# Two weight layouts per expert on TensorE, one expert after the other, and a ring of seven weight slots, in a decoder trunk with a mixture of experts

## The chip, the cores and the metric

The kernel runs on one core of one Trainium2 chip. The metric is the device time of one execution in microseconds; lower is better. Durations inside an execution come from one profiled execution, whose times are counted from its first instruction.

## The reference, cut to what matters

Two decoder layers work on 256 tokens of width 1024 in float32. Layer 0 has forgetting attention, layer 1 differential attention on shared keys and values; each ends in a mixture of 16 experts (grouped top 2) of hidden width 512.

```python
for l in range(2):
    ...                                     # ada parameters, attention, post-norm residual
    h = modulate(x, sh_f, sc_f)
    gates = ...                             # (256, 16), two non-zero entries in each row
    for e in range(16):
        a = silu(h @ w_gate[l, e]) * (h @ w_up[l, e])      # 1024 -> 512
        out = out + gates[:, e:e + 1] * (a @ w_down[l, e]) # 512 -> 1024
    x = post_norm_residual(x, out, g_f, ...)
```

Only the rows of h that were routed to an expert matter for it. The router's choices for the inputs of `setup_inputs()`, counted with the reference, are these numbers of tokens for experts 0 to 15:

| layer | tokens of experts 0 to 15 |
|---|---|
| 0 | 17 21, 18 24, 38 15, 38 21, 27 45, 84 40, 28 30, 37 29 |
| 1 | 43 18, 3 44, 16 9, 1 14, 44 38, 16 72, 25 33, 93 43 |

The commas part the pairs in which the kernel takes them. Ten experts of layer 0 and eight of layer 1 have at most 32 tokens; expert 10 of layer 0 and experts 11 and 14 of layer 1 have more than 64.

## The kernel before

**Weights.** All weights stream from HBM in pieces of 2 MB ([128, 4096] float32), issued by SP in one written order. A piece goes into one of `RING` = 6 slots of `ring`; in the expert stages two more slots, `spare` and `stream`, join. `SLOT` and `TURN` fix at build time which slot a piece takes: in the ring stages piece n takes the slot of piece n - 6, in the expert stages that of piece n - 8. SP issues piece n when the semaphore `used` of its slot says that the last piece there was read, and waits in order, so one full slot holds up all later pieces. An expert stage has 48 pieces, six for each pair of experts: gate and up of the first expert, gate and up of the second, then the two down matrices (numbers 6i to 6i + 5 for pair i). Pieces `RING` and `RING` + 1 of a stage also wait for `x_ready` and `res_mm`. In layer 0 the six slots before the expert stage hold the four pieces of `ada(3)`, read by `mod_product(3)` in the router's stage, and the two output projections.

**Routing and windows.** DVE's `route` makes one-hot selections, positions and tables; PE gathers the tokens, sorted by expert, into `xsT`. For each expert POOL's `window` copies 64 columns into `xw`. Tokens beyond 64 go through `overflow`, rounds of 32 in a loop whose count DVE, ACT, PE and POOL load from `tabn`. There POOL copies the window `oxw` and PE runs `gate_up_strips`: four strips of 32 output columns, two for gate and two for up, each with half of the contraction, folded together by a matmul with `fold_strips`.

**A pair on PE.** `gate_up` of the first expert (8 steps of two matmuls side by side on 64 columns each, two PE instructions for each float32 matmul), `gate_up` of the second; in its middle the four transposes of the first expert's result, so that ACT's sigmoid and DVE's `glu` of the first run beneath the second. Then four `add_back` matmuls of the pair before (L1737), the second's transposes, `down` of the first, the transposes of `put`, `down` of the second. DVE's `gated` multiplies the outputs by the adaLN gate into `y`, which the next pair adds back. After an expert stage PE needs `ada(4)`, the four pieces behind it in SP's order (`turn_stream(1)`, L1431), and after layer 1 the last norm and the store.

Lines: L498 expert loads, L618 and L613 POOL's overflow copies, L630 and L631 windows, L799 and L805 ACT's copies of gate and up, L802 and L808 sigmoids, L1225 `put_pair`, L1233 and L1235 `glu`, L1242 `gated`, L1247 to L1271 DVE's overflow, L1724 and L1725 `gate_up`, L1732 and L1733 `down`, L1746 and L1756 strips, L1773 fold, L1811, L1821 and L1828 transposes.

## Time and profile before

| | |
|---|---|
| median of 3 runs | 900.73 us (900.71 to 902.5) |
| span of the profiled execution | 899.3 us |
| PE busy | 834.7 us, 93% |
| DVE, ACT, POOL busy | 376.0, 127.1, 90.3 us |
| read from HBM | 302.49 MB |
| mean granted TensorE clock | 0.986 |

The profiled execution's own total is not listed; its span is 1.4 us below the median, and that is taken as what lies before the first and after the last instruction. A clock of 1.00 is 2.4 GHz and 0.50 is 1.2 GHz. The page cuts the span into 40 slices of 22.5 us; further views give the chain of work that ended last, the instructions in order of time, busy times by stretch, and groups by line.

### The profile page before, as it was taken

How to read it: one execution, taken by the hardware profiler on the slowest of the kernel's cores; microseconds unless marked ns; L12 is line 12 of the kernel's file. 1: busy time of each engine (PE TensorE's matmuls, PEld its weight loads, DVE VectorE, ACT ScalarE, POOL GpSimd, SP SyncE). 2: the span in 40 equal slices, each digit the busy share in tenths (PEclk: the TensorE clock that was granted, in tenths of full speed). 3: DMA queues.
4: the chain of work that ended last, by engine and by line, in shares of the span. 5: the costliest groups of instructions: out<-in, count | busy, mean ns of one | idle time of the engine just before them, and what ended most of it. 6: DMA issues, size and time to landing. Idle time of an engine off the chain costs nothing.

```text
span 899.3 us, 10792 instructions
## 1 busy us (share of the span) xinstructions
PE 834.7 (93%) x3730; PEld 393.0 (44%) x3730; DVE 376.0 (42%) x927; ACT 127.1 (14%) x341; POOL 90.3 (10%) x146
## 2 busy tenths in 40 slices
PE   6899999999998998899979999999999999889984
PEld 3584675435333333333328557654533333333331
DVE  2185867475211221222148688828521122212215
ACT  1001243011100000000010114611110000010010
POOL 1000000051110001011004000215111110000000
PEclk9999999999999999999999999999999999999998
DMA  8999982019999999999999799405499999999901
GB/s 352 431 421 426 399 329 95 1 59 431 426 428 426 425 427 426 427 426 426 425 384 419 299 426 425 175 0 213 163 406 424 428 424 427 426 427 426 392 12 47
DMA packets 23408, 304.59 MB, mean 339 GB/s; under 512 B 2720, under 2 KB 3232, under 8 KB 5280
## 3 DMA queue, kind: packets, MB, share of 16 engines
q1 hardware_dynamic: 22752, 303.14, 80.6%
q8 instruction: 47, 0.77, 0.3%
q10 hardware_dynamic: 576, 0.40, 0.1%
q14 instruction: 33, 0.27, 0.1%
HBM read 302.49 MB, written 1.05 MB: 338 GB/s over the span
## 4 chain that ended last, share of the span: by engine, by line
PE 68%; DMA 21%; DVE 8%; issue 2%; POOL 1%; ACT 1%; POOLq 0%; DVEq 0%; ACTq 0%
PE ps L1724 17%; DMA ring<-in_moe_w_up_dram 12%; PE ps L1732 7%; PE ps L1558 6%; PE ps L1529 6%; PE ps L1542 6%; PE ps L1642 5%; PE ps L1737 4%; DMA stream<-in_moe_w_up_dram 3%; DMA ring<-in_ada_w_dram 3%; DMA ring<-in_moe_w_down_dram 3%; PE ps L1453 1%; PE ps L1431 1%; PE ps L1705 1%; PE ps L1465 1%
## 5 line engine op out<-in xcount | busy, mean ns | idle before, releaser
L1724 PE MATMUL ps<-ring,hT 128*64 128x512 f32 x384 | 172.4, 599 | 11.8 <-DMA ring<-in_moe_w_up_dram 9.9
L1725 PE MATMUL ps<-ring,hT 128*64 128x512 f32 x384 | 172.7, 600 | 0.0
L1233 DVE TENSOR_TENSOR arena<-arena,ps 128x256 f32<-128x256 f32 x32 | 13.5, 421 | 233.8 <-ACT arena L802 126.8
L1724 PEld LDWEIGHTS ps<-ring,hT 128*64 128x64 f32 x384 | 51.1, 138 | 117.4 <-issue 117.4
L1732 PE MATMUL ps<-ring,arena 128*64 128x512 f32 x208 | 94.8, 599 | 0.0
L1733 PE MATMUL ps<-ring,arena 128*64 128x512 f32 x208 | 94.8, 598 | 0.0
L414 DVE SCALAR_TENSOR_TENSOR spare<-ring,csig,spare 128x512 f32<-128x512 f32 x112 | 86.1, 769 | 3.8
L1737 PE MATMUL ps<-arena 128*128 128x512 f32 x144 | 66.6, 605 | 3.2 <-DVE arena L1242 3.2
L1724 PE MATMUL ps<-spare,hT 128*64 128x512 f32 x128 | 58.9, 609 | 2.7 <-DMA stream<-in_moe_w_up_dram 2.5
L1725 PE MATMUL ps<-stream,hT 128*64 128x512 f32 x128 | 58.9, 610 | 0.0
L1529 PE MATMUL ps<-hT,ring 128*128 128x256 f32 x256 | 57.2, 386 | 1.5 <-ACT hT L680 1.5
L630 POOL COPY hT<-arena 128x512 f32 x32 | 19.7, 615 | 372.6 <-PE ps L1725 222.1
L1242 DVE TENSOR_TENSOR arena<-ps,gbc 64x512 f32<-64x512 f32 x64 | 43.9, 686 | 29.6 <-PE ps L1733 28.6
L1542 PE MATMUL ps<-ring,hT 128*128 128x512 f32 x128 | 55.9, 595 | 0.0
L1529 PEld LDWEIGHTS ps<-hT,ring 128*128 128x128 f32 x256 | 49.6, 194 | 8.5 <-ACT hT L680 1.6
L1725 PEld LDWEIGHTS ps<-ring,hT 128*64 128x64 f32 x384 | 51.2, 138 | 0.0
L1732 PEld LDWEIGHTS ps<-ring,arena 128*64 128x64 f32 x208 | 26.3, 136 | 48.9 <-issue 48.9
L1737 PEld LDWEIGHTS ps<-arena 128*128 128x128 f32 x144 | 25.9, 189 | 43.7 <-issue 43.7
L799 ACT ACTIVATE arena<-ps 128x512 f32<-128x512 f32 x16 | 9.6, 597 | 243.4 <-PE ps L1725 243.4
L1542 PEld LDWEIGHTS ps<-ring,hT 128*128 128x128 f32 x128 | 24.1, 190 | 30.8 <-issue 30.8
L1724 PEld LDWEIGHTS ps<-spare,hT 128*64 128x64 f32 x128 | 17.3, 140 | 38.7 <-issue 38.7
L587 POOL TENSOR_SCALAR st<-mv 128x1 f32<-128x1 f32 x8 | 1.8, 223 | 294.6 <-DVE mv L1064 294.6
(281 smaller groups left out, 1083.3 us busy)
## 6 DMA issues: line engine op xcount, KB each, us to landing
ring<-in_moe_w_down_dram SPq DMA_DIRECT2D x26, 2048.0 KB, 21.8
ring<-in_ada_w_dram SPq DMA_DIRECT2D x24, 2048.0 KB, 14.7
ring<-in_moe_w_gate_dram SPq DMA_DIRECT2D x24, 2048.0 KB, 18.4
ring<-in_moe_w_up_dram SPq DMA_DIRECT2D x24, 2048.0 KB, 21.3
spare<-in_moe_w_gate_dram SPq DMA_DIRECT2D x8, 2048.0 KB, 23.2
stream<-in_moe_w_up_dram SPq DMA_DIRECT2D x8, 2048.0 KB, 25.3
ring<-in_fox_w_in_dram SPq DMA_DIRECT2D x6, 2048.0 KB, 9.8
ring<-in_kv_ada_w_dram SPq DMA_DIRECT2D x4, 2048.0 KB, 13.8
```

The lines of the kernel that those rows point to most:

```text
L414: ins = alu.scalar_tensor_tensor(out=dst, in0=w[:, k, :], scalar=csig[:, k:k + 1], in1=dst, op0=ALU.mult, op1=ALU.add)
L630: link(g.tensor_copy(xw[:, j, :, 0:CAP], xsT[:, :, bass.ds(first, CAP)]))
L1242: d.tensor_tensor(out[lo:lo + CAP, half], ps[part_, bank, :], gbc[part_, 1, half], ALU.mult).then_inc(done, 1)
L1529: mm = t.matmul(ps[:, u % 4, 0:S], wcols(piece)[:, k, cc * P:(cc + 1) * P], src[:, k, :], start=(k == 0), stop=(k == KC - 1))
L1542: mm = t.matmul(ps[:, u % 4, :], hT[:, k, b * P:(b + 1) * P], wcols(piece)[:, k, :], start=(k == 0), stop=(k == KC - 1))
L1558: mm = t.matmul(ps[:, 7, 0:S], wcols(n)[:, k, (c % 4) * P:(c % 4 + 1) * P], src[:, k, :], start=(k == 0), stop=(k == KC - 1))
L1642: mm = t.matmul(ps[:, 2 * b + s_, :], oT[l][:, k, b * P:(b + 1) * P], wcols(n)[:, k, :], start=(k == 0), stop=(k == KC - 1))
L1724: t.matmul(ps[0:CAP, bank, :], lhs(k), wcols(ng)[:, k, :], start=(k == 0), stop=(k == KC - 1))
L1725: mm = t.matmul(ps[CAP:P, bank, :], lhs(k), wcols(nu)[:, k, :], start=(k == 0), stop=(k == KC - 1))
L1732: t.matmul(ps[0:CAP, bank, :], lhs(f), wdown(n)[:, f, 0:512], start=(f == 0), stop=(f == 3))
L1733: mm = t.matmul(ps[CAP:P, bank, :], lhs(f), wdown(n)[:, f, 512:D], start=(f == 0), stop=(f == 3))
L1737: return t.matmul(ps[:, 2 * b + q, :], lhs[:, b * P:(b + 1) * P], yy[:, q * 512:q * 512 + 512], start=False, stop=True, skip_group_check=True)
```

## The change

The ring gets a seventh slot, so a piece takes the slot of the piece seven before it, or nine before it in the expert stages. On PE each expert is now one chain: `gate_up`, add-backs or transposes of `put`, fold or transposes, add-backs, `down`; then the next expert. A table `tabl`, made in `route`, says which experts have more than 32 tokens. PE loads its entry and branches: these take the old instructions (64 columns), the others take strips of 32 columns in bank 4 or 5 and a fold by a 128-wide `folded`. Slots are released later in the chain: gate and up of the first expert by the first two add-backs, of the second by the `put` transposes and the fold. `put_pair` writes 8 half-wide pieces instead of 4. The copies into `oxw` move from POOL to DVE, and ACT and DVE do their parts in the new order. The routing tiles move into `arena`, and a scratch size is passed at the build.

```diff
--- before.py
+++ after.py
-RING = 6
+RING = 7
...
-        fold_strips = sb("fold_strips", [P, 2 * OCAP])
+        fold_strips = sb("fold_strips", [P, 2, CAP])
...
-        rt = sb("rt", [P, 11, NB * NE])
-        rg = sb("rg", [P, 6, 2 * 2 * 8])
-        rc = sb("rc", [P, 2, NB * NG * EG * EG])
+        rt = part(P, 11, NB * NE)
+        rg = part(P, 2, NB * NG)
+        rc = part(P, 2, NB * NG * EG * EG)
...
             def windows(l):
-                def overflow(i, j):
...
-                        with pool.Fori(b, b + n) as r:
-                            g.tensor_copy(oxw[:, :, 0:OCAP], xsT[:, :, bass.ds(lo, OCAP)]).then_inc(o_own, 1)
...
-                            pool.wait_ge(o_pe, r * 5 + 1)
...
                 def window(i, j, o):
-                    if i:
-                        spent(pool, N_MOE[l] + 6 * (i - 1) + 2 * j + 1)
+                    if i or l:
+                        pool.wait_ge(gu_mm[j], i + 8 * l)
...
@@ scalar, experts @@
+                    act.wait_ge(gu_mm[0], q + 1)
+                    a.activation(gu[:, 0, :], ps[:, 4, :], ACT.Copy).then_inc(gu_ev[0], 1)
                     overflow(i, 0)
-                    spent(act, n0 + 1)
-                    a.activation(gu[:, 0, :], ps[:, 4, :], ACT.Copy).then_inc(gu_ev[0], 1)
                     act.wait_ge(tg_mm[0], q + 1)
...
@@ vector, route @@
+                totals, past = rt[:, 7, 0:NE], rt[:, 7, NE:2 * NE]
+                link(d.tensor_tensor(totals, each[:, 0:NE], each[:, NE:2 * NE], ALU.add))
+                link(d.tensor_scalar(past, totals, float(OCAP), float(OCAP), ALU.is_gt, ALU.mult))
+                link(d.tensor_tensor(t3(2), pos[:, :, 0:NE], past.unsqueeze(1).broadcast_to([P, NB, NE]), ALU.subtract))
+                link(d.tensor_copy(tabl[:, :], past[0:1, :]))
...
-                link(d.tensor_tensor(tot, each[0:1, 0:NE], each[0:1, NE:2 * NE], ALU.add))
+                tot = totals[0:1, :]
...
@@ vector, experts: put_pair, overflow, pair loop @@
-                            d.tensor_scalar(put[:, b, j * CAP:(j + 1) * CAP], lane[:, :],
-                                            pos[:, b, bass.ds(i * 2 + j, 1)], gate[:, b, bass.ds(i * 2 + j, 1)],
+                            d.tensor_scalar(put[:, b, lo:lo + OCAP], lane[:, :], pos[:, b, e:e + 1], gate[:, b, e:e + 1],
                                             ALU.is_equal, ALU.mult).then_inc(putted, 1)
+                            d.tensor_scalar(put[:, b, lo + OCAP:lo + CAP], lane[:, :], second[:, b, e:e + 1],
+                                            gate[:, b, e:e + 1], ALU.is_equal, ALU.mult).then_inc(putted, 1)
...
+                            d.tensor_copy(oxw[:, :, 0:OCAP], xsT[:, :, bass.ds(lo, OCAP)]).then_inc(o_own, 1)
...
+                            d.tensor_copy(oxw[:, :, bass.ds(to, OCAP)], xsT[:, :, bass.ds(src_, OCAP)]).then_inc(o_win, 1)
...
                     overflow(i, 0)
                     put_pair(i)
                     glu(0, q)
+                    dve.wait_ge(sc_mm, i + (10 * l + 1))
+                    spent(dve, n0 + 4)
+                    gated(y, 0, 4, y_ev[0])
                     overflow(i, 1)
-                    glu(1, q)
-                    dve.wait_ge(sc_mm, i + (10 * l + 1))
                     dve.wait_ge(tp_mm, q + 1)
                     d.tensor_copy(putT[:, :], ps[:, 6, 0:S]).then_inc(tp_ev, 1)
-                    spent(dve, n0 + 4)
-                    gated(y, 0, 4, y_ev[0])
+                    glu(1, q)
...
@@ tensor, experts @@
+                def between(i, j, q, n0):
+                    if j == 0:
+                        pe.wait_ge(tp_ev, q + 1)
+                        pe.wait_ge(y_ev[1], (q + 1) * 2)
+                        add_back(0, 0, putT, y).then_inc(used[slot(n0)], 1)
+                        add_back(0, 1, putT, y).then_inc(used[slot(n0 + 1)], 1)
+                    else:
+                        pe.wait_ge(putted, (q + 1) * 8)
+                        for b in range(NB):
+                            mm = t.transpose(ps[:, 6, b * P:(b + 1) * P], put[:, b, :], ident[:, :])
+                            if b == 0:
+                                mm.then_inc(used[slot(n0 + 2)], 1)
+                        mm.then_inc(tp_mm, 1)
+                    pe.wait_ge(gu_ev[j], q + 1)
+                def ahead_of_down(i, j, q, n0):
+                    if j == 0:
+                        add_back(1, 0, putT, y)
+                        add_back(1, 1, putT, y).then_inc(sc_mm, 1)
+                    pe.wait_ge(at_r[j], q + 1)
+                    landed(pe, n0 + 4 + j)
...
+                    for j in range(2):
+                        pe.wait_ge(y_ev[j], (q + 1) * 2)
+                        landed(pe, n0 + 2 * j)
+                        landed(pe, n0 + 2 * j + 1)
+                        pe.wait_ge(xw_r[j], q + 1)
+                        large = pe.value_load(tabl[0:1, bass.ds(i * 2 + j, 1)], min_val=0, max_val=OCAP)
+                        with pe.If(large > 0):
+                            gate_up(i, j, lambda k: xw[:, j, k, 0:CAP], 4 + j, range(KC)).then_inc(gu_mm[j], 1)
+                            overflow(i, j)
+                            between(i, j, q, n0)
+                            for f in range(4):
+                                mm = t.transpose(ps[:, 4 + j, f * P:(f + 1) * P], gu[:, j, f * P:(f + 1) * P], ident[:, :])
+                                if j and not f:
+                                    mm.then_inc(used[slot(n0 + 3)], 1)
+                            mm.then_inc(tg_mm[j], 1)
+                            ahead_of_down(i, j, q, n0)
+                            down(i, j, lambda f: aT[:, j, f * CAP:(f + 1) * CAP], 4 + j).then_inc(used[slot(n0 + 4 + j)], 1)
+                        with pe.Else():
+                            gate_up_strips(i, j, xw[:, j, :, :], 4 + j).then_inc(gu_mm[j], 1)
+                            between(i, j, q, n0)
+                            for f in range(4):
+                                mm = t.matmul(ps[:, 4 + j, f * P:(f + 1) * P], gu[:, j, f * P:(f + 1) * P], folded,
+                                              start=True, stop=True)
+                                if j and not f:
+                                    mm.then_inc(used[slot(n0 + 3)], 1)
+                            mm.then_inc(tg_mm[j], 1)
+                            ahead_of_down(i, j, q, n0)
+                            down_strips(i, j, aT[:, j, :].rearrange("p (c s) -> p c s", c=4), 4 + j
+                                        ).then_inc(used[slot(n0 + 4 + j)], 1)
...
-    nc = _bacc.Bacc("TRN2", target_bir_lowering=False, num_devices=1)
+    nc = _bacc.Bacc("TRN2", target_bir_lowering=False, num_devices=1, dynamic_dma_scratch_size=1024)
```

## Rows read from the trace of the kernel before

**Rows 1.** The page: busy times, then GB/s in 40 slices of 22.5 us.
```profile
PE 834.7 (93%) x3730; PEld 393.0 (44%) x3730; DVE 376.0 (42%) x927; ACT 127.1 (14%) x341; POOL 90.3 (10%) x146
...
GB/s 352 431 421 426 399 329 95 1 59 431 426 428 426 425 427 426 427 426 426 425 384 419 299 426 425 175 0 213 163 406 424 428 424 427 426 427 426 392 12 47
```

**Rows 2.** The chain that ended last: start us, length us, what it waited on.
```profile
349.29 25.07 DMA ring<-in_moe_w_down_dram
...
433.99 26.35 DMA ring<-in_ada_w_dram
...
643.79 0.61 PE ps L1724
...
756.94 27.44 DMA ring<-in_moe_w_up_dram
...
885.58 1.97 PE ps L1737 x4
```

**Rows 3.** Busy time by stretch: PE, PEld, DVE, ACT, POOL, clock, DMA share, GB/s.
```profile
652.00:784.00 132.00, 129.48 (x566) 45.75 (x562) 30.00 (x75) 11.08 (x21) 13.11 (x22) 1.00 1.00 422
```

**Rows 4.** SP's queue in order of time: start us, length us, what was issued.
```profile
117.00 25.01 SPq L484 DMA_DIRECT2D ring<-in_fox_w_o_dram  x2
197.49 0.33 SPq L498 DMA_DIRECT2D ring<-in_moe_w_gate_dram  x1
...
642.91 0.33 SPq L498 DMA_DIRECT2D stream<-in_moe_w_up_dram  x1
651.76 0.33 SPq L498 DMA_DIRECT2D ring<-in_moe_w_gate_dram  x1
```

**Rows 5.** The chain again, transposes of the first expert in two pairs that follow.
```profile
680.38 0.59 PE ps L1811 x4
...
706.46 0.59 PE ps L1811 x4
```

**Rows 6.** One of these pairs in order of time, all engines, cut.
```profile
680.32 0.66 PE L1811 MATMUL ps<-ident,arena 128*128 128x128 f32 x4
...
681.88 0.42 DVE L1235 TENSOR_TENSOR arena<-arena,ps 128x256 f32<-128x256 f32 x1
...
692.14 0.44 PE L1828 MATMUL ps<-ident,arena 128*128 128x128 f32 x2
...
692.50 0.64 PE L1732 MATMUL ps<-ring,arena 128*64 128x512 f32 x1
...
695.99 0.59 PE L1724 MATMUL ps<-ring,hT 128*64 128x512 f32 x1
```

**Rows 7.** An overflow round of layer 1 in order of time, cut.
```profile
794.07 3.64 PE L1746 MATMUL ps<-ring,mrow 128*32 128x512 f32 x32
...
797.78 0.60 ACT L785 ACTIVATE mrow<-ps 128x512 f32<-128x512 f32 x1 [6.80 <-PE ps L1746]
...
798.51 1.10 PE L1773 MATMUL ps<-fold_strips,mrow 128*128 128x64 f32 x8 [0.80 <-ACT mrow L785]
...
806.24 3.70 PE L1737 MATMUL ps<-arena 128*128 128x512 f32 x8
```

**Rows 8.** Order of time: two waits for weights; then 1 us as in rows 3.
```profile
340.38 0.61 PE L1724 MATMUL ps<-ring,hT 128*64 128x512 f32 x1 [2.74 <-DMA ring<-in_moe_w_up_dram]
...
784.62 0.61 PE L1724 MATMUL ps<-ring,hT 128*64 128x512 f32 x1 [3.04 <-DMA ring<-in_moe_w_up_dram]
...
786.00:787.00 1.00, 1.00 (x5) 0.33 (x3) 0.00 (x0) 0.00 (x0) 0.00 (x0) 0.50 1.00 426
```

**Rows 9.** Order of time: two loaded branches, and the last overflow's down strips.
```profile
641.76 1.28 ACT L799 ACT_TABLE_LOAD   x1 [0.69 <-issue]
...
645.74 0.54 DVE L1225 TENSOR_SCALAR arena<-lane,pos,gate 128x64 f32<-128x64 f32 x2 [1.53 <-issue]
...
857.59 3.50 PE L1756 MATMUL ps<-ring,fold 128*32 128x512 f32 x16 [1.03 <-DVE fold L1267]
```

**Rows 10.** Order of time: DVE's third copy of gathered tokens in layer 1.
```profile
639.43 0.81 DVE L898 TENSOR_SCALAR arena<-ps,modc 128x512 f32<-128x512 f32 x1 [0.51 <-PE ps L1705]
```

114 lines of the change are left out of this document (38 added, 76 removed).

## The prediction

> **What bounds the kernel now.** I read the page first: PE is busy 93% of the span, and the transfers run at 424 to 428 GB/s through both expert stages [rows 1]. Both look full, so the chain of waits has to say which one ends last, and where. In layer 0 it is the transfers. The chain waits there on one piece of weights after another, on the first down matrix of pair 5 (lands at 374.36) and at the end on the last piece of `ada(4)` (433.99 + 26.35 = 460.34) [rows 2]. In layer 1 the wait that matters is at 756.94 + 27.44 = 784.38, when the up matrix of pair 5's second expert (piece 33 of 48) lands [rows 2]. Up to there the transfers run full [rows 3]; behind it PE is the bound until the last add-back at 885.58 [rows 2]. Between the layers (460 to 644) the chain is PE and DVE work and waits for no transfer.
>
> So two prices have to be kept apart: a piece of 2.097 MB at 426 GB/s takes 4.92 us, 29.5 us per pair [rows 1], and a pair on PE takes 706.46 - 680.38 = 26.1 us [rows 5]. PE is faster already. Work taken from PE is worth time only behind the last wait for weights, in pairs 5 to 7 of layer 1.
>
> **The seventh slot.** In layer 0 SP issues the second projection piece at about 142 (117.00 + 25.01), then waits to 197.49 for `mod_product(3)` to free a slot [rows 4]. The slices from 135 to 197 are nearly empty [rows 1]. With seven slots the first expert piece takes the slot of a query piece, the one that the projection got at 142, and lands in that gap. At 197.5 the queue is one piece ahead and stays so, because the stage is bound by transfers to its end: `ada(4)` lands at 455.4, 4.9 earlier, and layer 1 starts 4.9 earlier. The cover for this is that PE finishes the stage by 455. With the prices below: pair 5's first down matrix lands at 374.4 - 4.9 = 369.5, the rest of expert 10 and its round takes 13.4, expert 11 13.4, pairs 6 and 7 19 and 24, the last gating and add-backs 5.3, so 444.6 and eleven us of room. If PE came later than 455, the gain would shrink by the excess.
>
> **Start of layer 1.** PE starts at 643.79 [rows 2]; now 643.8 - 4.9 + 0.4 = 639.3. The 0.4 is for `route`: three more small DVE operations of 0.16 to 0.2 us with their links, 0.65 in all, ahead of the copies of gathered tokens; a later copy waits 0.51 for PE [rows 10], so part is hidden (bounds 0 and 0.65). Before, SP issued piece 8 at 651.76 [rows 4], 8.0 behind PE's start, when a slot came free. Now pieces 0 to 8 are in by then, and piece 9 waits for the first add-back: load and branch 0.5, `gate_up` 7.0, add-back 0.9, so 639.3 + 8.4 = 647.7. Before, it took 784.4 - 651.8 = 132.6 us from that issue to the landing 26 pieces later. The same count now runs from piece 9 to piece 34, pair 5's first down matrix: 780.3. One more stall: piece 11 waits for expert 1's `put` transposes at about 658.5, and the two pieces before it are read by 658.9, an issue taking some 1.4 us to move data; I add 1.1. Piece 34 lands at 781.5. Before, at 4.92 behind piece 33, it would have been 789.3.
>
> **Prices on PE.** `down` on 64 columns takes 695.99 - 692.50 = 3.5 us and `gate_up`, twice as many matmuls, 7.0; four transposes 0.7; eight add-back instructions 3.7, so half of them 1.8; from the transposes' end over sigmoid and `glu` to PE 1.4 (680.98 to 682.30, and a wake-up) [rows 6]. The strips were already measured in the overflow: 3.64 for gate and up, then 0.8 until ACT's copy frees PE, 1.1 for the fold; the whole round delays the add-backs by 12.2 (794.07 to 806.24) [rows 7]. Down strips I price at 1.9: the one row shown took 3.50 at half clock [rows 9], and half the columns' time of `down` is 1.75. The wider fold stays at 1.1 (8 instructions of 0.14; above, at most twice that). So a small expert saves 3.4 + 1.6 and pays 0.4 for the fold.
>
> **The chain by expert costs some of this.** For the first expert of a pair the two add-backs cover ACT's copy and the other two cover sigmoid and `glu`. For the second nothing does: 0.8 for the copy (the `put` transposes lie inside it) and 1.4 ahead of `down` are now exposed, where before the neighbour's matmuls hid them. Two large experts cost 7.0 + 1.8 + 0.7 + 1.8 + 3.5 and 7.0 + 0.8 + 0.7 + 1.4 + 3.5, together 28.2, 2.1 more than before; two small ones 10.2 + 8.8 = 19, seven less; one of each 23 to 24.
>
> **Load and branch.** No row shows PE loading a value with an empty queue. Two loads and a branch cost ACT 0.69 and DVE 1.53 [rows 9]. One load and a longer jump on PE I take as 0.5, nearest to ACT's row; bounds 0 and 1.5. Behind a large expert PE's queue covers it, as it covers two loads after `gate_up` today (the old round starts without a gap); behind strips or a wait for weights it is exposed.
>
> **Edits at nothing.** The copies of `oxw` move to DVE, which has them done before PE leaves `gate_up`: after `gated` (1.4), two loads (1.5), two copies of about 0.4 and two more loads (1.5), 5 us against 7.5; if that cover went, a round would grow by the excess. The eight operations of `put_pair` and DVE's checks (some 5.4 us behind a pair) come ahead of the next `glu`, which PE reaches 7 us behind it. POOL loses its loop and its loads; its windows were 14 us ahead. Moved tiles and the scratch size issue no instruction.
>
> **The tail of layer 1.** PE's arrival: pair 4's first down matrix lands at 781.5 - 29.5 = 752.0; 0.3 to wake, 1.6 for half clock, 3.5, then expert 9 with 13.4 gives 770.8, expert 10 up to its `down` 8.3 gives 779.1. So PE still waits 2.4 us for piece 34. From there:
> - `down` of expert 10: 0.3 + 1.6 + 1.9 = 3.8
> - expert 11 (72 tokens): 0.5 + 7.0 + 12.4 + 0.4 + 0.7 + 1.4 + 3.5 = 25.9 (12.4: the round with its wider fold)
> - expert 12 (25): 0.5 + 3.6 + 1.8 + 1.1 + 1.8 + 1.9 = 10.7
> - expert 13 (33): 0.5 + 7.0 + 0.8 + 0.7 + 1.4 + 3.5 = 13.9
> - expert 14 (93): 7.0 + 12.4 + 1.8 + 0.7 + 1.8 + 3.5 = 27.2
> - expert 15 (43): 7.0 + 0.8 + 0.7 + 1.4 + 3.5 = 13.4
>
> That is 94.9. One more stretch at half clock, as the old tail had one in its last overflow [rows 9], adds 1.6: 96.5, so PE's last `down` ends at 878.0. From there to the last add-backs is 1.6, and from these to the end of the span 899.3 - 885.6 = 13.7. The span is 893.3. Before, the same stretch took 99.4 from the landing at 784.6, so the change gains mostly by the earlier weights and little by strips: four of the last six experts are large and two overflow. Outside the span lie 900.73 - 899.3 = 1.4 us: **894.7 us**.
>
> **The rivals.**
> - *PE's order shows none of these costs.* No half clock in the tail (-3.2), loads hidden (-1.5 and -0.5 at the start), no stall at piece 11 (-1.1): 888.4. For it: large queues hide such things today. Against: the gaps of 0.80 and more in the old rounds [rows 7]. Chance 0.15.
> - *The clock.* After an idle of 2.74 us, at 340, PE's matmuls kept their length; after one of 3.04, at 784, the granted clock stood at 0.50, which is 1.2 GHz, from 786 on [rows 8], which lost about 1.6. The new chain has more waits, within experts and for weights. Three more such stretches in the tail give 894.7 + 4.8 = 899.5, which is no change. Chance 0.15. The Trainium skill (TensorE: Matmul & The Clock Gate, section Loop structure matters more than you think) calls it bad to wait for a transfer between matmuls, since they then run cold. By that rule each of the waits in pairs 0 to 5 costs; the trace agrees at 786 and not at 340.
> - *Control flow, the slower side.* PE pays 1.5 us at every expert, large ones too, as DVE does [rows 9]: in the tail six times 1.5 in place of three times 0.5 (+7.5), 1.0 at the stage's start, and experts 9 and 10 use up the 2.4 of waiting (+0.6): 903.8. It decides from about 1 us per expert more than I take, since six experts then eat the 6 us of gain. For it: the jump passes much more code than any today. Against: no gap at PE's present branches. Chance 0.12.
> - *The slot brings nothing*, because another wait of SP holds the first expert piece: then 4.9 of the gain and the share in layer 1 go, about 900.7. SP's row shows only the slot as releaser. Chance 0.03.
>
> **How the numbers follow.** The forecast has 0.55; its own range is 891 to 899, from the bounds of load, fold and landing. The range 888 to 902 takes in the first two rivals and leaves the third out. What a measurement of this kernel can tell from no change is about 0.2%, 1.8 us: faster means below 898.9, slower above 902.5. Faster: 0.52 of the forecast, 0.15, and 0.05 of the clock's case, 0.72; same: 0.03, 0.10 and 0.03, 0.16; slower 0.12.
>
> **What would show it.** Right: one expert piece issued at about 142 and not at 197; `ada(4)` landed at 455; the first gate matmul of layer 1 at 639; PE waiting for pair 5's first down matrix to about 781, and hardly any wait behind that; small experts' gate and up in 3.6 us. Wrong: idle PE ahead of each expert with no releaser (control flow), long rows at 0.50 in pairs 5 to 7 (clock), transfers below 420 GB/s from 650 to 780 (slots released too late by the new order), or a layer 0 that PE ends later than 455.

## The result, and the profile after

The changed kernel takes 906.35 us (median of 10 runs, 899.99 to 910.73), the kernel before beside it 902.15 (10 runs, 896.89 to 903.27). The ratio is 1.0055, with a 95% interval of 1.0035 to 1.0075: 0.55% slower. The forecast was 894.7, 0.7% faster, with a range that ended at 902. The profiled execution took 902.39 us with a span of 900.6, so it is 4 us quicker than the median of its kernel and shows only a part of the loss.

The page, cut: busy times, GB/s in 40 slices of 22.5 us, and the queue that carries the engines' instructions (packets, MB, share).

```profile
PE 773.7 (86%) x3802; PEld 368.0 (41%) x3802; DVE 394.2 (44%) x1005; ACT 124.6 (14%) x339; POOL 88.0 (10%) x139
...
GB/s 355 431 419 430 428 384 95 1 64 430 424 426 426 425 425 426 425 417 422 417 391 428 305 424 427 171 0 219 156 307 428 426 423 427 424 426 427 362 48 47
...
q8 instruction: 63, 1.03, 0.5%
```

PE has 61 us less to do than before [rows 1] and ends no sooner. The queue of instructions moved 63 packets; in the kernel before it was 47:

```profile
q8 instruction: 47, 0.77, 0.3%
```

The page's list of line groups says what became of the 61 us, and the view of PE's waits sums it (line, what it waited for, us in total, times, longest):

```profile
PE ps L1749 <- issue: 38.3, 15, 7.5
...
PE ps L1727 <- issue: 4.6, 2, 3.2
```

Together 42.9 us in 17 gaps: 25.8 us in layer 0 and 17.1 in layer 1. "Issue" is idle time that no semaphore and no transfer ends. L1749 are the strips of gate and up, L1727 the 64 columns. Where in the program such a gap lies is seen in PE's rows in order of time:

```profile
241.92 0.60 PE L1749 MATMUL ps<-ring,hT 128*32 128x512 f32 x2
241.93 0.59 PE L1749 MATMUL ps<-spare,hT 128*32 128x512 f32 x1
245.98 0.62 PE L1749 MATMUL ps<-spare,hT 128*32 128x512 f32 x1 [3.45 <-issue]
...
333.78 1.07 PE L1749 MATMUL ps<-ring,hT 128*32 128x512 f32 x2 [7.47 <-issue]
```

The first of these two gaps stands in the middle of one expert's run of strips, with 14 of its matmul records in front of it. Between two strips of a run there is no wait, no load and no branch. So it isn't data that PE lacks; whether it is the next instruction, the experiments have to show. The chain that ended last shows what the gaps did (start, length, what):

```profile
276.04 35.02 DMA ring<-in_moe_w_down_dram
...
326.31 7.47 issue
...
459.22 3.67 PE ps L1740 x8
462.89 4.43 PE ps L1432 x40
...
645.20 0.94 issue
...
758.27 33.06 DMA spare<-in_moe_w_down_dram
791.47 1.96 PE ps L1759 x16
...
886.94 1.97 PE ps L1740 x4
```

The last add-back of layer 0 ends at 462.89, and `mod_product(4)` (L1432) follows on it without waiting for `ada(4)`: PE, not the transfers, ends layer 0, 2.4 us later than in the chain before (460.48). Layer 1 starts at 646.14 instead of 643.79, piece 34 is read at 791.47, and the last add-backs start at 886.94 instead of 885.58 [rows 2]. The slot did its own part: the first expert piece is issued at 141.80 instead of 197.49 [rows 4].

### The profile page after: what moved, and what is told of

The parts are those of the page before. It is cut to its first block, busy times and chain, and to the rows that moved or that the text cites. A ratio compares the mean times of both kernels' runs of the same rounds, so it can differ in the third digit from the quotient of the medians.

```text
span 900.6 us, 10801 instructions
## 1 busy us (share of the span) xinstructions
PE 773.7 (86%) x3802; PEld 368.0 (41%) x3802; DVE 394.2 (44%) x1005; ACT 124.6 (14%) x339; POOL 88.0 (10%) x139
## 3 DMA queue, kind: packets, MB, share of 16 engines
HBM read 302.49 MB, written 1.05 MB: 337 GB/s over the span
## 4 chain that ended last, share of the span: by engine, by line
PE 67%; DMA 11%; DVE 11%; issue 6%; ACT 2%; DVEq 1%; POOL 1%; ACTq 0%; POOLq 0%; SPq 0%
PE ps L1749 9%; PE ps L1727 7%; PE ps L1559 6%; PE ps L1530 6%; PE ps L1543 6%; PE ps L1740 5%; PE ps L1643 5%; PE ps L1735 5%; DMA ring<-in_moe_w_down_dram 4%; PE ps L1759 4%; DMA spare<-in_moe_w_down_dram 4%; DMA spare<-in_moe_w_up_dram 3%; PE ps L1844 2%; PE ps L1454 1%; PE ps L1432 1%
## 5 line engine op out<-in xcount | busy, mean ns | idle before, releaser
L1749 PE MATMUL ps<-ring,hT 128*32 128x512 f32 x496 | 83.0, 690 | 33.1 <-issue 33.1
L1727 PE MATMUL ps<-ring,hT 128*64 128x512 f32 x160 | 72.4, 606 | 6.4 <-issue 4.6
L1728 PE MATMUL ps<-ring,hT 128*64 128x512 f32 x176 | 77.7, 594 | 0.0
L1740 PE MATMUL ps<-arena 128*128 128x512 f32 x144 | 69.2, 605 | 3.2 <-DVE arena L1232 3.2
L1749 PEld LDWEIGHTS ps<-ring,hT 128*32 128x32 f32 x496 | 20.0, 122 | 87.7 <-issue 87.6
L1735 PE MATMUL ps<-ring,arena 128*64 128x512 f32 x80 | 38.1, 621 | 11.1 <-DVE arena L1225 7.1
L1727 PEld LDWEIGHTS ps<-ring,hT 128*64 128x64 f32 x160 | 21.8, 140 | 55.8 <-issue 55.8
L1736 PE MATMUL ps<-ring,arena 128*64 128x512 f32 x80 | 38.2, 622 | 0.0
L1291 DVE COPY arena<-ps 128x256 f32<-128x256 f32 x16 | 6.8, 424 | 71.1 <-PE ps L1803 71.1
L1759 PE MATMUL ps<-ring,arena 128*32 128x512 f32 x224 | 28.5, 629 | 9.7 <-DVE arena L1225 9.7
L780 ACT ACTIVATE arena<-ps 128x512 f32<-128x512 f32 x16 | 9.6, 598 | 190.9 <-PE ps L1749 109.3
L786 ACT ACTIVATE arena<-ps 128x512 f32<-128x512 f32 x16 | 9.6, 597 | 168.5 <-PE ps L1749 90.9
L1214 DVE TENSOR_SCALAR arena<-lane,pos,gate 128x32 f32<-128x32 f32 x64 | 19.0, 296 | 27.2 <-issue 22.6
```

The lines of the kernel that those rows point to most:

```text
L1727: t.matmul(ps[0:CAP, bank, :], lhs(k), wcols(ng)[:, k, :], start=(k == 0), stop=(k == KC - 1))
L1728: mm = t.matmul(ps[CAP:P, bank, :], lhs(k), wcols(nu)[:, k, :], start=(k == 0), stop=(k == KC - 1))
L1735: t.matmul(ps[0:CAP, bank, :], lhs(f), wdown(n)[:, f, 0:512], start=(f == 0), stop=(f == 3))
L1740: return t.matmul(ps[:, 2 * b + q, :], lhs[:, b * P:(b + 1) * P], yy[:, q * 512:q * 512 + 512], start=False, stop=True, skip_group_check=True)
L1749: mm = t.matmul(ps[OCAP * s_:OCAP * (s_ + 1), bank, :], src[:, k, 0:OCAP], wcols(ng + s_ // 2)[:, k, :], start=(kk == 0), stop=(kk == 3))
L1759: mm = t.matmul(ps[OCAP * s_:OCAP * (s_ + 1), bank, :], src[:, f, 0:OCAP], wdown(n)[:, f, 512 * q:512 * q + 512], start=(ff == 0), stop=(f ...
```

## The experiments

All ratios are to the kernel before, run on the same chip in turn, with 95% intervals. "Built" means that the choice between 64 columns and strips is made when the program is built, from the token counts of this input. "Old order" is PE's order as before the change, "chain" the changed kernel's order by expert.

| kernel | order | small experts on | slots | us | ratio |
|---|---|---|---|---|---|
| changed | chain | strips, branch | 7 | 906.35 | 1.0055 [1.0035, 1.0075] |
| e2_static | chain | strips, built | 7 | 897.7 | 0.9963 [0.9937, 0.9988] |
| e11_static_load | chain | strips, built, load kept | 7 | 898.23 | 0.9968 [0.9941, 0.9996] |
| e5_swapped | chain | strips, branch turned round | 7 | 911.13 | 1.0118 [1.0072, 1.0164] |
| e4_split | chain | strips, short branches | 7 | 899.61 | 0.9966 [0.9945, 0.9986] |
| e3_chain64 | chain | 64 columns | 7 | 913.79 | 1.0127 [1.0100, 1.0154] |
| e6_reorder | chain | strips, built, pieces in chain order | 7 | 894.87 | 0.9940 [0.9919, 0.9961] |
| e16_static_ring6 | chain | strips, built | 6 | 907.88 | 1.0088 [1.0065, 1.0110] |
| e1_ring7 | old | 64 columns | 7 | 890.5 | 0.9879 [0.9853, 0.9905] |
| e13_ring7_again | old | 64 columns | 7 | 887.27 | 0.9861 [0.9835, 0.9886] |
| e9_dead72 | old | 64 columns, 290 dead instructions | 7 | 1019.46 | 1.1295 [1.1245, 1.1345] |
| e10_dead24 | old | 64 columns, 96 dead instructions | 7 | 903.62 | 1.0022 [1.0000, 1.0045] |
| e14_ring7_ov | old | 64 columns, copies on VectorE | 7 | 896.02 | 0.9958 [0.9939, 0.9977] |
| e12_inter64 | old | 64 columns, other parts of the change | 7 | 898.82 | 0.9973 [0.9949, 0.9997] |
| e7_inter_static | old | strips, built | 7 | 895.34 | 0.9950 [0.9929, 0.9970] |
| e8_inter_split | old | strips, short branches | 7 | 897.25 | 0.9964 [0.9947, 0.9981] |
| e15_inter_pool | old | strips, built, copies on GpSimd | 7 | 889.17 | 0.9875 [0.9851, 0.9899] |

Differences below are worked out from the ratios, at 900.45 us for the kernel before. Two ratios together leave some 3 us open, so a difference of 2 us or less is not told from none.

**The choice made when the program is built.**

```diff
-    large = pe.value_load(tabl[0:1, bass.ds(i * 2 + j, 1)], ...)
-    with pe.If(large > 0):
+    if i * 2 + j in LARGE[l]:
...
-        overflow(i, j)
+        if i * 2 + j in OVER[l]:
+            overflow(i, j)
...
-    with pe.Else():
+    else:
```

> The changed kernel with the choice between 64 columns and strips made when the program is built, from the token counts of this input (so the kernel holds these counts and isn't a general one): no load, no branch, no code that is jumped over, overflow code only for the three experts that have overflow. Order, strips and slot stay. Theory A (jumps): the idle time that the trace ends with nothing but issue goes, 26 us in layer 0 and 17 in layer 1; layer 0 is bound by transfers again, ada(4) lands at 455 to 456, PE waits for pair 5's first down matrix to about 781; time 889 to 897. Rival B (the chain by expert, with its exposed copy, sigmoid and glu, eats the gain): the gaps may go, but the time stays at 900 or above. Rival C (PE loses by the low clock behind its waits for data, not at the jumps): rows at a clock of 0.50 stay as many as in the changed kernel, mean clock 0.967, time over 900.

It took 897.7 us, 8.3 below the changed kernel. No gap with "issue" is left at the experts, and the queue of instructions moved 30 packets instead of 63 for the same 3802 matmul records:

```profile
q8 instruction: 30, 0.49, 0.2%
```

But the 42.9 us didn't come back as time. PE's waits of this kernel, the larger ones for transfers:

```profile
PE ps L1761 <- DMA ring<-in_moe_w_down_dram: 16.6, 3, 7.4
PE ps L1761 <- DVE arena L1227: 12.5, 9, 1.4
...
PE ps L1737 <- DMA ring<-in_moe_w_down_dram: 8.1, 3, 4.4
PE ps L1434 <- DMA ring<-in_ada_w_dram: 6.4, 1, 6.4
```

In all PE waits 48.8 us for transfers of weights here (the nine rows of the view that name a weight tensor and 0.8 us or more), and 6.5 in the changed kernel, which has 42.9 of "issue". By these totals the gaps mostly stand where PE would have waited for weights, and what they cost is the 8.3 us by which they overrun. The two profiled executions show 5.0 of it: layer 1 starts at 642.57 instead of 646.14, and the last add-backs start at 881.87 instead of 886.94. So the theory of the jumps holds for these 8.3, and the time of 897.7, just outside what it expected, says that something else holds the rest. The mean granted clock is 0.962, no higher than with the branch (0.967): the low clock that theory C names stays, so it is not the jumps' alone.

**The load alone.** The same, with the load of the table value put back and its value unused.

> The kernel that chooses when it is built (897.7), with the changed kernel's load of the table value put back on PE for every expert, its value unused: no branch and nothing jumped over. Theory A (the load is cheap, the jump is dear): at most 0.5 us per expert, and only behind strips and waits for weights, so 898 to 902 with gaps of 0.5 at most. Rival (loading a value through an empty queue is what takes 2 to 3.5 us): as the changed kernel, 904 to 908.

898.23 us, 0.5 more than without, which is inside the noise, and no gap. The load is cheap, as the prediction had it; what is dear is the branch that passes code.

**The branch turned round.** Strips in the `If`, 64 columns with the overflow code in the `Else`.

```diff
-    with pe.If(large > 0):
-        (64 columns, overflow)
-    with pe.Else():
-        (strips)
+    with pe.If(large < 1):
+        (strips)
+    with pe.Else():
+        (64 columns, overflow)
```

> The changed kernel with the two bodies of its branch exchanged: strips in the If, 64 columns with the overflow code in the Else. Nothing else moves, and as many instructions are jumped over in all. Theory A1 (PE gets its instructions in blocks, in the order in which they stand, and code that is jumped over has to be fetched too: 63 blocks of 16 KB in the changed kernel, 30 in the one that chooses when it is built): the long stretch now stands behind the strips, whose 10 us of matmuls and waits hide its fetch; gaps with the releaser issue fall from 43 us to under 20, time 898 to 903. Theory A2 (the taken jump itself empties PE, wherever it stands): the gaps only move to the start of the expert behind a small one, 904 to 908.

911.13 us: slower still, and theory A1 missed; A2 had the place right and the time 3 us too low. Now the gaps stand at the start of the expert that follows a small one, mostly large ones:

```profile
PE ps L1727 <- issue: 30.3, 9, 5.7
...
PE ps L1749 <- issue: 12.4, 5, 4.3
```

42.7 us again. Ten us of strips ahead of the jump hide nothing of it, so what is passed isn't fetched far enough ahead while PE works. The total is that of the changed kernel; more of it lies in the tail, where no transfer covers it (2.71 us at 795.39 and 4.31 at 837.50, against 2.67 at 821.50).

**Dead code by dose.** To price the jump by itself, the kernel with the slot alone (below) got code that is never entered, ahead of each expert's overflow check; nothing more is executed than the comparison.

```diff
+    with pe.If(n > 4):
+        for _ in range(72):        # 24 in the other
+            t.matmul(ps[0:CAP, 6, :], xw[:, j, 0, 0:CAP], wcols(...)[:, 0, :], start=True, stop=True)
     with pe.If(n > 0):
```

> The kernel before with the seventh slot (890.5), and for every expert, ahead of its overflow, a branch that is never entered over 72 dead matmul calls, about 290 of PE's instructions, as long as the stretch that the changed kernel jumps over for a small expert. It executes no more work. Theory A (passing 290 instructions that aren't executed costs PE 2.4 us: 43 us at 18 small experts in the changed kernel): 32 experts give 77 us, of which layer 0 can hide some 7 of waits for weights and the last expert none; 940 to 965. Rival (the gaps come from loading the value or from waking an empty queue, the jump is free): 890 to 893.

> The same with 24 dead calls, about 96 instructions per expert. Theory A in its form with a reach (PE's supply of instructions runs some way ahead of it; a jump within that is free, as the kernel before jumps over some 150 at each expert without a gap): within 4 us of 890.5. Theory A in its form by amount (what is passed has to be fetched, 2.4 us per 290 instructions): 0.8 us per expert, 32 x 0.8 = 26, so 910 to 917. Rival (the jump is free): 890 to 893.

72 dead calls: 1019.46 us, 129 above the slot alone (e13), more than expected. PE's waits:

```profile
PE ps L1737 <- issue: 55.4, 14, 4.6
PE ps L1724 <- issue: 40.4, 13, 3.8
...
PE ps L1725 <- issue: 0.7, 1, 0.7
```

At the 32 jumps there are 29 gaps, most of 3 to 4.6 us, 97 in all. Some 43 more are PE's own: it is busy 874.1 us for 3730 records, against 830.7 without the dead code, because it runs at a granted clock of 0.50 (1.2 GHz) behind many of the gaps: eight add-back matmuls take 5.40 us there, 3.67 elsewhere. In return 6.5 us of waits for weights are gone. The queue of instructions moved 83 packets:

```profile
q8 instruction: 83, 1.36, 0.5%
```

These are 36 more than the slot alone: 32 x 72 / 36 = 64 calls, some 256 instructions, to a packet. So dead code is fetched too.

The expectation passed over one thing in this edit: the overflow's own branch, over some 150 instructions, follows with no matmul between. So an expert without overflow passes some 440 instructions here and some 250 with 24 calls, not 290 and 96. In the slot alone, which passes the 150 by themselves, PE's rows show no gap with "issue" at the experts.

24 dead calls: 903.62 us, 14.5 above the slot alone, and 59 packets, 12 more. Per dead instruction that is a third of the price of 72, and it isn't spread: the trace has six gaps, 17.0 us in all, the largest of the old size (start, length, ..., idle before).

```profile
264.64 4.64 PE L1737 MATMUL ps<-arena 128*128 128x512 f32 x5 [4.07 <-issue]
...
836.27 5.40 PE L1737 MATMUL ps<-arena 128*128 128x512 f32 x8 [3.93 <-issue]
```

Both forms of theory A missed in part: neither free within a reach nor proportional, but some jumps pay in full and most pay nothing. That fits a supply in packets: passing 150 in one go left no gap, 250 left six at 32 experts, 290 (the changed kernel) 17 at 18 small ones, and 440 left 29 at 32. In the Trainium skill (Runtime: NRT & Kernel Launch, section Instruction fetch mechanics) it is stated that instructions are fetched in blocks of 256, in sequence, and that a taken branch to a target outside the present two blocks stalls until that block is fetched. The runs agree in the size of a packet and in the kind of step between 150 and 290; the page has no duration, and these traces give mostly 1 to 4.6 us, and up to 7.5.

**Short jumps.** Three `If` and `Else` per expert, around gate and up, the transposes and `down` alone; overflow and add-backs outside.

```diff
     with pe.If(large > 0):
         gate_up(...)
-        overflow(i, j)
-        between(i, j, q, n0)
-        ...
+    with pe.Else():
+        gate_up_strips(...)
+    overflow(i, j)
+    between(i, j, q, n0)
+    with pe.If(large > 0):
+        (transposes)
+    with pe.Else():
+        (fold)
+    ...
```

> The changed kernel with the same choice at run time, but with short jumps: one load, then three If and Else around gate and up alone, around the four transposes alone and around down alone; the overflow with its own branch and the add-backs stand outside. Theory A, in the form that a jump over much code empties PE's supply of instructions (the changed kernel passes some 290 instructions for each small expert, this one at most some 70 at a time): the gaps of 2.3 to 3.5 us go, what is left is some 0.2 to 0.5 us per taken branch where PE has nothing queued; 892 to 900. Theory A in the other form, that any taken jump empties PE, whatever its length: this kernel takes three to four times as many, so it is slower than the changed kernel, 910 or more. Rival B: as the changed kernel, 904 to 908.

899.61 us, as theory A in its first form expected, 0.3 above the choice made when the program is built and 8 below the changed kernel, though it takes three jumps where that takes one. "Any taken jump" falls. Of the large gaps four are left, all in layer 0 (2.35 to 3.49 us), and small ones of 0.2 to 0.6. It fetched 62 packets, so it isn't the amount of code either, but how much is passed at once.

**The slot alone.**

```diff
-RING = 6
+RING = 7
...
-        rt = sb("rt", [P, 11, NB * NE])
...
+        rt = part(P, 11, NB * NE)
...
-    nc = _bacc.Bacc("TRN2", target_bir_lowering=False, num_devices=1)
+    nc = _bacc.Bacc("TRN2", target_bir_lowering=False, num_devices=1, dynamic_dma_scratch_size=1024)
```

> The kernel before with the seventh ring slot alone (with the tiles moved and the scratch size that make room for it); PE's order, the 64 columns and the branches stay. Theory A (in the changed kernel PE idles at the jumps to the strips, some 26 us in layer 0 and 17 in layer 1, and eats what the slot gives): the slot alone is worth most of one piece, 4.9 us, in layer 0, because PE of before keeps up with the transfers: the last piece of ada(4) lands at about 455.5 instead of 460.3, layer 1 starts 4 to 5 earlier, time 896 to 898. Rival D (the slot brings nothing, or costs something elsewhere, and PE's jumps are innocent): within 1.5 us of before or slower.

> The kernel before with the seventh slot alone, once more, beside the next three on one chip. If the 11 us are the slot's: 889 to 892 again. If part of it was chance: 893 to 897, which is what the prediction's 4.9 us give.

890.5 and, in the second run, 887.27 us: 10.9 and 12.5 faster than before, more than twice the 4.9 expected, and the best of all. (The moved tiles and the scratch size go with the slot here; the run with six slots below keeps both and prices the slot by itself.) It beats both kernels. Its chain (e13):

```profile
429.90 25.30 DMA ring<-in_ada_w_dram
455.33 4.50 PE ps L1431 x40
...
636.97 0.61 PE ps L1724
...
871.90 1.97 PE ps L1737 x4
```

The last piece of `ada(4)` lands at 455.20, 5.1 earlier than in the chain before, where 455.4 was predicted. But the matmuls behind it take 4.50 us, and before they took more:

```profile
460.48 6.20 PE ps L1431 x40
```

That is the kernel before: PE had waited 3.75 us for the piece and ran at 0.52 of its clock from 462 to 465; here it waited 1.85 and stayed at 1.00. This is 1.7 us that no step of the prediction had seen, so layer 1 starts 6.8 earlier. Layer 1 then takes 234.9 us instead of 241.8: PE meets piece 33 without a wait (3.04 before [rows 8]) and so without the half clock behind it (1.6), and the half clock in the last overflow [rows 9] is gone as well (1.5); together 6.1 of the 6.9. The last of these is not the slot's for certain: in the first run (e1) the low clock stands in the first overflow round of layer 1 instead, whose down strips take 3.12 us there and 1.97 in e13.

**The chain on 64 columns.** Every expert on 64 columns, no branch. (The two halves of `put` are left as they are in the changed kernel, so small experts' outputs are counted twice; no operation is added or left out by that.)

> The changed kernel with every expert on 64 columns, chosen when the program is built: chain by expert and slot stay; strips (but for the overflow's own), load and branch are gone. 18 small experts then cost 3.4 us more for gate and up, 1.6 more for down and 0.4 less for the fold, 4.6 each. Theory A with the prices of the prediction: a pair takes 28.2 us on PE and a transfer-bound pair 29.5, so PE still nearly keeps up; in layer 0 PE becomes the bound with its one overflow round, some 2 to 5 us later than without it; in the tail only expert 12 differs (4.6). Time 4 to 10 above the kernel without branches that keeps its strips: 897 to 904. Rival C (transfers bind all, strips are worth nothing): within 2 us of that kernel. If it lies above 908, the chain by expert itself costs more than was priced.

913.79 us, 13.9 above the same parts in the old order (e12) and 14.8 above the chain with strips. No transfer is waited for at the experts; the price of the chain stands in PE's waits:

```profile
PE ps L1737 <- DVE arena L1227: 22.9, 18, 1.6
...
PE ps L1835 <- ACT arena L788: 4.9, 15, 0.3
```

L1737 is `down` behind `glu`, 1.38 for the second expert of each pair, L1835 the transposes behind ACT's copy. 27.8 us in 16 pairs, 1.7 per pair, where 2.1 were predicted. So strips gain 14.8 in an order that loses 13.9.

**Pieces in the chain's order.** SP sends gate, up and down of one expert, then of the other.

```diff
-    e = 2 * i + (j // 2 if j < 4 else j - 4)
-    w = (moe_w_gate, moe_w_up, moe_w_down)[j % 2 if j < 4 else 2]
+    e = 2 * i + j // 3
+    w = (moe_w_gate, moe_w_up, moe_w_down)[j % 3]
```

> The kernel that chooses when it is built (so for this input's token counts alone), with the weights sent in the order in which the chain by expert reads them: gate, up and down of the pair's first expert, then those of the second; before and after the change the two down matrices come last. Theory E (chain and transfers are out of step: PE asks for the fifth piece of a pair when it has read two, and the slot of a down matrix that is read early stays empty until the piece in front of it finds its own): the waits for the first down matrix, 4.45, 3.42, 4.72 us in layer 0 and 7.39, 4.40, 3.61 in layer 1, mostly go; 3 to 6 us below the kernel with the old sending order, 891 to 895. Rival (only the rate of the transfers counts, the waits move to the next piece): 896 to 899.

894.87 us, 2.1 below the old sending order by the ratios, which is not told from none, and less than the 3 to 6 expected. The waits for `down` pieces are gone and stand now at gate and up (12.9 + 11.6 + 11.2 + 4.0) and at `ada(4)` (9.8): they moved to the next pieces, as the rival said, so the sending order is worth little.

**Six slots under the chain.**

> Chain by expert and strips chosen when the program is built, but six slots as before. Theory E (the chain asks for a pair's fifth piece two pieces early, so it lives on the ring's depth): the waits for the first down matrix grow by up to 4.9 us each, and the time by 8 to 14 over the same with seven slots (897.7): 905 to 912. Rival (the slot is worth one piece and no more): 901 to 904.

907.88 us, as theory E expected: the slot by itself is worth 11.3 here too. Layer 0 ends 4.8 later (`ada(4)` lands at 462.08 and not at 457.29), and layer 1 takes 6.0 us more (892.20 - 646.90 = 245.3, against 881.87 - 642.57 = 239.3). The mechanism that theory E gave is not what the trace shows: PE's waits for down matrices grow only from 31.7 to 35.2 us in all.

**Strips in the old order.** PE's order as before, strips for small experts.

```diff
     (pair, in the order as before)
-    gate_up(i, 0, ...)
+    if 2 * i in LARGE[l]:
+        gate_up(i, 0, ...)
+    else:
+        gate_up_strips(i, 0, ...)
     ... (the same at gate and up of the second, the transposes and both downs)
```

> Strips for small experts chosen when the program is built (this input's token counts alone), seventh slot and overflow copies on VectorE, but PE's order as before the change: both experts' gate and up, then add-backs, transposes, both downs. Theory B+E (the chain by expert is what eats the gain, by 1.75 us per pair of exposed copies, sigmoids and glus and by asking for down matrices early): against the kernel with the slot alone (890.5) layer 0 stays, bound by transfers, ada(4) landing at about 454; in layer 1 PE has 8 x 4.6 = 37 us less to do and is bound by the last pieces, which land at about 837, with some 10 to 15 us of work behind them; time 864 to 876. Rival (transfers bind both, strips bring nothing in any order): 886 to 892.

> The same order as the kernel before, slot and strips, with the choice at run time: two loads per pair and seven short If and Else around single operations, the overflow with its own branch. Theory A1 (instructions come in blocks, skipped ones too; short jumps are nearly free as long as PE has work queued and the blocks keep up): 2 to 8 us above the same order with the choice made when the program is built, from branches behind waits and from single gaps of 2 to 3.5 us at block ends in layer 0 (where the weights' transfers hide them): 868 to 882. Theory A2 (each taken jump costs 1 to 1.5 us): five taken jumps per pair, 8 pairs, 40 to 60 us in layer 1: 900 or above.

895.34 us built and 897.25 with short branches. The second is 1.3 above the first by the ratios, less than the 2 to 8 expected and inside the noise; but both lie far above the 864 to 876 that I expected of strips. The step that failed was mine here: I let layer 1 end behind the last transfer. PE waits for piece 33 until 780.34, at the rate of the transfers, and the 99 us of work from there to the last add-back belong to six experts, four of them large and two with overflow; of the two small ones one has its gate and up already behind it. The prediction had said so of the tail, and the expectation forgot it.

**What came with the strips.** Both kernels lie above the slot alone. The next three ask why.

```diff
-    (GpSimd) g.tensor_copy(oxw[:, :, 0:OCAP], xsT[:, :, bass.ds(lo, OCAP)]).then_inc(o_own, 1)
+    (VectorE) d.tensor_copy(oxw[:, :, 0:OCAP], xsT[:, :, bass.ds(lo, OCAP)]).then_inc(o_own, 1)
```

> PE's order as before, seventh slot, every expert on 64 columns, no choice; but with the changed kernel's other parts: overflow copies on VectorE, put in two halves, the wider fold, three more operations in the routing. Theory F (strips bring nothing in this order since the transfers bind, and cost a clock drop where PE then waits; the 4.8 us that the strips' kernel in this order lies above the slot alone are the overflow copies, which PE waited 3.4 us for at one round, and the routing): 892 to 896, within 2 us of the one with strips. Rival (strips are what costs the 4.8): 889 to 891.

> The seventh slot and the overflow copies on VectorE in place of GpSimd; nothing else of the change. Theory F (in the order as before the copies come late, since VectorE has other work ahead of them: 3.4 us at one of the two rounds of layer 1, and the clock falls behind that wait): 3 to 6 us above the slot alone. Rival (the 8 us come from put in halves, the routing's three operations and the wider fold): within 1.5 us of the slot alone.

> Strips for small experts chosen when the program is built (this input's token counts alone), PE's order as before, seventh slot, overflow copies on GpSimd as before. Theory F: without the late copies this lies 3 to 6 us below the one with VectorE's copies (895.3): 889 to 892, so that strips in the old order are worth no more than 2 us beside the slot alone. Rival (the copies are innocent): 894 to 897.

e12 (all 64 columns, with the change's other parts) took 898.82, more than either side expected, so strips aren't what costs; e14 (the slot, and the overflow copies on VectorE alone) 896.02, 8.7 above the slot alone, where theory F had 3 to 6. PE's row for the first round of layer 1, and the stretch behind `ada(4)` (columns as in [rows 3]), both of e14:

```profile
790.23 5.33 PE L1738 MATMUL ps<-ring,mrow 128*32 128x512 f32 x32 [3.38 <-DVE mrow L1248]
```

```profile
456.00:459.00 3.00, 1.20 (x8) 0.45 (x12) 1.90 (x5) 0.00 (x0) 0.79 (x2) 0.50 0.99 421
459.00:462.00 3.00, 3.00 (x16) 0.67 (x12) 0.76 (x2) 0.00 (x0) 0.00 (x0) 0.50 0.97 410
```

In the old order VectorE has other work ahead of the copies: PE waits 3.38 and runs the round's strips at half clock, 5.33 instead of 3.64, 5.1 in all. The other part is at `ada(4)`, which lands at 457.66, 2.5 later than in e13; PE waits 4.14 for it, the clock falls, and the 40 matmuls take 6.86. Of the 2.5 us, 0.6 are there when the stage starts; what the other 1.9 come from stays open. e15, with the copies back on GpSimd, took 889.17, as theory F expected, and 1.3 above the slot alone, which is not told from none: strips in the old order bring nothing that these runs can show. They take 3.7 us off layer 1 (231.2 against 234.9), but PE waits 11.5 us for `ada(4)`, whose matmuls then take 6.33, and layer 1 starts at 642.55 instead of 636.97:

```profile
PE ps L1442 <- DMA ring<-in_ada_w_dram: 11.5, 1, 11.5
```

## Why the prediction was wrong

Step by step, as it was laid out.

- *What bounds the kernel.* Right. Work taken from PE is worth time only behind the last wait for weights: strips in the order as before show no gain beside the slot (e15 against e13).
- *Load and branch, 0.5 us.* This step failed. The load is that cheap (e11: 0.5 us for the whole kernel). The jump isn't: 17 gaps of 42.9 us in all, 2.5 on the mean, with 18 small experts. They cost 8.3 us of the time (the changed kernel against e2). Without the branch the forecast would have been close: e2's 897.7 is 3.0 above it and inside the narrower range of 891 to 899. The rows of ACT and DVE that gave the price [rows 9] pass other lengths of code on other engines, and "no gap at PE's present branches", the argument against the rival, was true of jumps over some 150 instructions and was carried to one of some 290. With e9 and e10 (440 and 250 in one go) the gaps set in between 150 and 290. The prediction noted that the jump passes much more code than any in the kernel and then bounded its price by rows of short ones.
- *Layer 0, "eleven us of room".* Failed with it. PE was to be done at 444.6; it was done at 462.89, with 25.8 us of gaps in layer 0. The slot's 4.9 us went there: the prediction's own sentence, that the gain shrinks by the excess over 455, gives a loss of 7.5, and 462.89 is 2.4 later than the 460.48 before. Without gaps (e2) PE is done at 451, so 12 of the 18 us are theirs, and `ada(4)` lands at 457.29, near the 455.4 said.
- *Start of layer 1.* 646.14 instead of 639.3: 7.5 for layer 0, less 1.8 since `mod_product(4)` now runs at full clock, and 0.9 for the gap at 645.20 make 645.9. This term of the clock was missing: those matmuls ran at half clock behind the wait for `ada(4)` before the change (6.20 instead of 4.50), which wasn't read in its chain. In e2, PE waits 6.38 and they take 7.14.
- *Landing of piece 34, and the sum.* It landed at 791.33 instead of 781.5: 6.8 of the 9.8 us are the start of layer 1, 3.0 came up within it, where 17.1 us of gaps stand. PE reaches it 0.3 before it lands, not 2.4. With the tail below, which is 2.6 shorter than said, that makes the span 900.6 instead of 893.3. Outside the span lie 1.8 us instead of 1.4, and the profiled execution is 4.0 below the median.
- *The slot.* Its mechanism was right (issued at 141.80, `ada(4)` at 455.20 in e13), its size too small. The 4.9 were for layer 0; with its share in layer 1 the rival that the slot brings nothing makes it 6.0 (900.7 less 894.7). It is 11.3 in the chain (e2 against e16) and 10.9 and 12.5 by itself, where the traces also show stretches of low clock and PE's last wait for weights gone. The rival that the slot brings nothing falls.
- *Prices on PE.* They held: strips 3.64, down strips 1.92, fold 1.05 to 1.16, `glu` ahead of the second `down` 1.38. The chain's price held, 1.7 per pair for 2.1. From piece 34 to the last add-backs the tail was to take 96.5 + 1.6 = 98.1 and takes 886.94 - 791.47 = 95.5, and 95.7 without gaps (e2).
- *Edits at nothing.* The copies of `oxw` were covered in the chain (PE waits 1.6 us for them in three rounds), as said. In the old order they aren't, which no step had to ask.
- *The clock.* A rival with 0.15, that the chain's waits cost half-clock stretches, is a part of the truth: the mean granted clock is 0.967 after 0.986. The rule of the Trainium skill that the prediction cites (TensorE: Matmul & The Clock Gate, section Loop structure matters more than you think) speaks of a long wait between every matmul, and the prediction read it of any wait. The rows at `ada(4)` agree with it only behind the longer waits: the same 40 matmuls take 4.50 behind a wait of 1.85, and 6.20 to 7.14 behind waits of 3.75 and more.
- *The rival that came true.* "Control flow, the slower side" gave 903.8 and had a chance of 0.12. Its place differs: it has 1.5 us at every expert, large ones too; the gaps come with the long jumps, 38.3 us at the strips and 4.6 at two large experts that follow small ones, and short jumps leave few (e4). Its chance should have been set by the one fact named for it.

By the ratios, then: the slot gains 12.5 (e13), the other parts that go with the strips lose 10.1 (e12 against e13; 8.7 for the copies on VectorE alone in the old order), the chain by expert loses 13.9 (e3 against e12), the strips win 14.8 (e2 against e3), and the branch loses 8.3 (the changed kernel against e2): 5.0 slower in all. These are steps along one path, not prices to be added in another order: strips win 14.8 in the chain and nothing that shows in the old order, and most of what each part gives or takes ends in a wait for weights. What the copies on VectorE cost within the chain wasn't run by itself; PE waits 1.6 us for them there.

## What to carry to other kernels

Price a branch on PE by the length of code that it passes, together with any jump right behind it, and compare it only with branches of that length; keep an alternative short, or choose around single operations, where the loop body is long. Before several edits are made together, ask which one moves the bound: here one slot more gave 11 to 12.5 us, and the 61 us less that PE had to do were mostly paid out as waiting, for instructions or for weights. A wait that is removed may be worth more than its length, because the matmuls behind it run at the full clock.

## What the runs showed of the hardware

- PE stalls when it jumps over much code in one go. Some 150 instructions left no gap; some 250 left six gaps at 32 experts (0.7 to 4.2 us); some 290 left 17 gaps with 18 small experts (0.9 to 3.5 us, once 7.5); some 440 left 29 at 32 experts (most of 3 to 4.6 us). The stall can come some matmuls behind the jump.
- Code that isn't executed is fetched all the same. With the same 3802 matmul records the queue of instructions moved 30 packets when the choice was built and 63 with the branch; with the same 3730 it moved 47 without dead code, 59 with 24 dead calls per expert and 83 with 72.
- Behind a wait of 1.85 us at `ada(4)` the granted clock was 1.00 (2.4 GHz), behind 4.14 us it was 0.50 (1.2 GHz), and the same 40 matmuls took 4.50 and 6.86 us.
